# Six stages of a two-block transformer kernel, each with its moving tiles at another place in SBUF

## The reference, cut to what matters

```python
def swiglu(x, w_in, w_out):                       # twice, D_FF = 2816
    gate, up = jnp.split(x @ w_in, 2, axis=-1)
    return (jax.nn.silu(gate) * up) @ w_out

def sq_relu_mlp(h, up, down):                     # twice, D_FF_2 = 4096
    return jnp.square(jax.nn.relu(h @ up)) @ down

def conformer_conv(h, pw1, pw1_b, dw, dw_b, ln_w, ln_b, pw2, pw2_b):
    u = jax.nn.glu(h @ pw1 + pw1_b, axis=-1)
    ...                                           # 31 taps per channel, layer norm
    return jax.nn.silu(u) @ pw2 + pw2_b
```

## The kernel before

| tile | role | address | modulo 2048 |
|---|---|---|---|
| xn_hi, xn_lo | moving, up parts | 18560, 34944 | 128, 128 |
| w_hi, w_lo | stationary, block k of a slot at + 512 k | 67712, 84096 | 128 (then 640, 1152, 1664, 128, ...) |
| hid_hi, hid_lo | moving, down parts of all four layers | 125056, 157824 | 128, 128 |
| q_parts | queries; moving in the mixer's output product | 137344 | 128 |
| k_hi, k_lo | moving in the first mixer's scores | 170112, 182400 | 128, 128 |
| cy_hi, cy_lo | moving in pw2 | 125056, 141440 | 128, 128 |
| cu_hi, cu_lo | moving in the taps, first window | 162176, 166528 | 384, 640 |

## Time and profile before

### The profile page before, as it was taken

How to read it: one execution, slowest core, us unless ns; L and a number is a source line. 1 busy time by engine, 2 the same in 40 slices (tenths; PEclk the granted TensorE clock), 3 DMA queues, 4 the chain that set the end, 5 groups by cost and what they waited for, 6 DMA issues and landing times.

```text
span 2358.6 us, 36961 instructions
## 1 busy us (share of the span) xinstructions
PE 2303.7 (98%) x13968; PEld 1903.3 (81%) x13968; DVE 1165.4 (49%) x1781; ACT 910.2 (39%) x1444; POOL 1163.4 (49%) x685
## 2 busy tenths in 40 slices
PE   8999999999999999999999899999999999999998
PEld 7888887888888888878876678888888887888887
DVE  5432146268634421376554546723735986731632
ACT  5332125467743321265553314222233435222222
POOL 5444445554565454445374415444445983444442
PEclk9999999999999999999999989999999999999999
DMA  4323323310033333232110003332232232322321
GB/s 165 98 98 98 98 89 108 124 55 1 10 108 98 98 98 97 90 118 88 55 55 29 29 2 99 98 98 95 93 97 92 90 107 74 98 97 97 98 91 61
DMA packets 56125, 200.08 MB, mean 85 GB/s; under 512 B 6224, under 2 KB 6480, under 8 KB 56016
## 3 DMA queue, kind: packets, MB, share of 16 engines
q1 hardware_dynamic: 54432, 195.82, 25.7%
q10 hardware_dynamic: 1584, 2.75, 0.4%
HBM read 196.45 MB, written 2.10 MB: 84 GB/s over the span
## 4 chain that ended last, share of the span: by engine, by line
PE 50%; DVE 3%; ACT 1%; issue 0%; POOL 0%; DVEq 0%; POOLq 0%; ACTq 0%
PE ps L133 15%; PE ps L135 14%; PE ps L134 14%; PE ps L1997 1%; PE ps L640 1%; PE ps L1973 0%; DVE ps L2837 0%; PE ps L1993 0%; PE ps L655 0%; PE ps L1936 0%; PE ps L2044 0%; PE ps L1862 0%; DVE sb_aq L1002 0%; PE ps L1958 0%; DVE sb_ak_lo L1006 0%
## 5 line engine op out<-in xcount | busy, mean ns | idle before, releaser
L114 POOL TENSOR_TENSOR sb_w_lo<-sb_w_raw,sb_w_hi 128x1024 fp32r<-128x1024 f32 (+1 forms) x361 | 888.4, 2463 | 925.6 <-ACT sb_w_hi L101 923.9
L133 PE MATMUL ps<-sb_xn_hi,sb_w_hi 128*128 128x512 f32 x1688 | 666.5, 395 | 2.4 <-POOL sb_w_lo L224 2.4
L134 PE MATMUL ps<-sb_xn_lo,sb_w_hi 128*128 128x512 f32 x1688 | 658.1, 390 | 0.0
L135 PE MATMUL ps<-sb_xn_hi,sb_w_lo 128*128 128x512 f32 x1688 | 657.8, 390 | 0.0
L101 ACT ACTIVATE sb_w_hi<-sb_w_raw 128x1024 fp32r<-128x1024 f32 x362 | 380.4, 1056 | 476.6 <-PE ps L135 450.5
L133 PEld LDWEIGHTS ps<-sb_xn_hi,sb_w_hi 128*128 128x128 f32 x1688 | 316.6, 188 | 72.8 <-issue 3.6
L135 PEld LDWEIGHTS ps<-sb_xn_hi,sb_w_lo 128*128 128x128 f32 x1688 | 316.7, 188 | 67.6
L134 PEld LDWEIGHTS ps<-sb_xn_lo,sb_w_hi 128*128 128x128 f32 x1688 | 316.8, 188 | 66.2 <-issue 1.7
L133 PE MATMUL ps<-sb_hid_hi,sb_w_hi 128*128 128x512 f32 x864 | 336.3, 389 | 2.0 <-DVE sb_hid_lo L401 2.0
L135 PE MATMUL ps<-sb_hid_hi,sb_w_lo 128*128 128x512 f32 x864 | 336.1, 389 | 0.0
L134 PE MATMUL ps<-sb_hid_lo,sb_w_hi 128*128 128x512 f32 x864 | 336.1, 389 | 0.0
(11 more groups left out here) (444 smaller groups left out, 3010.2 us busy)
## 6 DMA issues: line engine op xcount, KB each, us to landing
sb_w_raw<-weights SPq DMA_DIRECT2D x365, 512.0 KB, 3.4
sb_stage<-x SPq DMA_DIRECT2D x4, 512.0 KB, 4.9
sb_abias<-table ACTq DMA_DIRECT2D x8, 256.0 KB, 3.8
out<-sb_out_stage SPq DMA_DIRECT2D x8, 256.0 KB, 2.9
sb_lora_w<-lora ACTq DMA_DIRECT2D x2, 256.0 KB, 2.8
sb_par<-params SPq DMA_DIRECT2D x1, 231.0 KB, 6.4
sb_ctaps<-dw ACTq DMA_DIRECT2D x1, 124.0 KB, 2.0
```

What stands on the lines that cost most here:

```text
L114: pool.tensor_tensor(c.w_lo[:, slot, 0:width], c.w_raw[:, slot, 0:width], c.w_hi[:, slot, 0:width].bitcast(F32), ALU.subtract).then_inc(c. ...
L133: pe.matmul(out, hi, rhs_hi(k0 + k), start=first, stop=False)
L134: pe.matmul(out, hi, rhs_lo(k0 + k), start=False, stop=False)
L135: mm = pe.matmul(out, lo, rhs_hi(k0 + k), start=False, stop=last)
```

## The change

Nothing is computed in another way and no instruction is added, removed or moved: each engine's list has the same operations, shapes and waits in the same order. What changes is where tiles lie. The four layers get hidden tiles of their own (`c.hid[name]`), which share one place in turn, each behind a gap of its own. `gate`, `h` and `out_stage` now stand ahead of the hidden tiles instead of behind them. A gap stands ahead of `q_parts` and one ahead of the convolution's tiles.

```diff
+HID_GAPS = (("ffn1", 1920), ("ffn2", 512), ("mlp0", 1024), ("mlp1", 64))
...
+    sb("gap_q", [P, 384])
     m.q = sb("q_parts", [P, 16, T], F32R)
...
+    sb("gap_cy", [P, 32])
     v.y_hi = sb("cy_hi", [P, KD, T], F32R)
...
-            c.hid_hi = sb("hid_hi", [P, F1A, T], F32R, region)
-            c.hid_lo = sb("hid_lo", [P, F1A, T], F32R, region)
             c.gate = sb("gate", [P, 2, T], scope=region)
             c.h = sb("h", [P, 2, T], scope=region)
             c.out_stage = sb("out_stage", [P, TT, D], scope=region)
+            c.hid = {}
+            for name, gap in HID_GAPS:
+                with ExitStack() as own:
+                    sb("gap_" + name, [P, gap // 4], scope=own)
+                    c.hid[name] = (sb(name + "_hid_hi", [P, F1A, T], F32R, own), sb(name + "_hid_lo", [P, F1A, T], F32R, own))
...
-                down_pe(pe, c, B[name + "_downA"], F1A, c.hid_hi, c.hid_lo, hid_ready(f))
+                down_pe(pe, c, B[name + "_downA"], F1A, *c.hid[name], hid_ready(f))
```

More of the change, by code:

```diff
@@ L378, in glu_up_act, with glu_up_dve @@
                 act.activation(c.gate[:, s // 2], c.ps[:, slot], ACT.Silu).then_inc(c.s_act, 1)
-def glu_up_dve(dve, c, base, nf, hid_base, act_base, free_pe):
+def glu_up_dve(dve, c, base, nf, hid_base, act_base, free_pe, hid):
     dve.wait_ge(c.s_pe, free_pe + START)
@@ L394, in glu_up_dve, with hidden_parts @@
             dve.wait_ge(c.s_evac, i * RING + (u + START + 1))
-            hidden_parts(dve, c, i, f, hid_base)
-def hidden_parts(dve, c, i, f, hid_base):
-    dve.tensor_copy(c.hid_hi[:, i * 2 + f], c.h[:, f]).then_inc(c.s_hhi, 1)
+            hidden_parts(dve, c, i, f, hid_base, hid)
+def hidden_parts(dve, c, i, f, hid_base, hid):
+    hid_hi, hid_lo = hid
+    dve.tensor_copy(hid_hi[:, i * 2 + f], c.h[:, f]).then_inc(c.s_hhi, 1)
     dve.wait_ge(c.s_hhi, i * 2 + (hid_base + f + 1))
-    dve.tensor_tensor(c.hid_lo[:, i * 2 + f], c.h[:, f], c.hid_hi[:, i * 2 + f].bitcast(F32),
+    dve.tensor_tensor(hid_lo[:, i * 2 + f], c.h[:, f], hid_hi[:, i * 2 + f].bitcast(F32),
                       ALU.subtract).then_inc(c.s_hid, 1)
@@ L2533, in mlp_up_act, with mlp_up_dve @@
             act.activation(c.gate[:, s % 2], c.ps[:, slot], ACT.Relu).then_inc(c.s_act, 1)
-def mlp_up_dve(dve, c, base, nf, hid_base, act_base):
+def mlp_up_dve(dve, c, base, nf, hid_base, act_base, hid):
+    hid_hi, hid_lo = hid
     dve.wait_ge(c.s_pe, base + START)
@@ L2546, in mlp_up_dve @@
             dve.wait_ge(c.s_evac, i * RING + (u + START + 1))
-            dve.tensor_copy(c.hid_hi[:, i * RING + s], c.h[:, s % 2]).then_inc(c.s_hhi, 1)
+            dve.tensor_copy(hid_hi[:, i * RING + s], c.h[:, s % 2]).then_inc(c.s_hhi, 1)
             dve.wait_ge(c.s_hhi, i * RING + (hid_base + s + 1))
-            dve.tensor_tensor(c.hid_lo[:, i * RING + s], c.h[:, s % 2], c.hid_hi[:, i * RING + s].bitcast(F32),
+            dve.tensor_tensor(hid_lo[:, i * RING + s], c.h[:, s % 2], hid_hi[:, i * RING + s].bitcast(F32),
                               ALU.subtract).then_inc(c.s_hid, 1)
@@ L3195, in ffn @@
                 up_pe(pe, c, B[name + "_upA"], 2 * F1A, KD * i, lambda: norm_pe(pe, c, i))
-                down_pe(pe, c, B[name + "_downA"], F1A, c.hid_hi, c.hid_lo, hid_ready(f))
+                down_pe(pe, c, B[name + "_downA"], F1A, *c.hid[name], hid_ready(f))
                 up_pe(pe, c, B[name + "_upB"], 2 * (F1 - F1A), KD * i, None)
-                down_pe(pe, c, B[name + "_downB"], F1 - F1A, c.hid_hi, c.hid_lo, hid_ready(f + F1A))
+                down_pe(pe, c, B[name + "_downB"], F1 - F1A, *c.hid[name], hid_ready(f + F1A))
             def mlp(name, f, i):
                 up_pe(pe, c, B[name + "_upA"], F1A, KD * i, lambda: norm_pe(pe, c, i))
-                down_pe(pe, c, B[name + "_downA"], F1A, c.hid_hi, c.hid_lo, hid_ready(f))
+                down_pe(pe, c, B[name + "_downA"], F1A, *c.hid[name], hid_ready(f))
                 up_pe(pe, c, B[name + "_upB"], F1A, KD * i, None)
-                down_pe(pe, c, B[name + "_downB"], F1A, c.hid_hi, c.hid_lo, hid_ready(f + F1A))
+                down_pe(pe, c, B[name + "_downB"], F1A, *c.hid[name], hid_ready(f + F1A))
             input_pe(pe, c)
@@ L3228, in ffn @@
                 norm_dve(dve, c, i)
-                glu_up_dve(dve, c, B[name + "_upA"], F1A, f, f, B[name + "_upA"])
+                glu_up_dve(dve, c, B[name + "_upA"], F1A, f, f, B[name + "_upA"], c.hid[name])
                 down_dve(dve, c, B[name + "_downA"], F1A, 0.5, scaled)
-                glu_up_dve(dve, c, B[name + "_upB"], F1 - F1A, f + F1A, f + F1A, B[name + "_upB"])
+                glu_up_dve(dve, c, B[name + "_upB"], F1 - F1A, f + F1A, f + F1A, B[name + "_upB"], c.hid[name])
                 layer_end_dve(dve, c, B[name + "_downB"], F1 - F1A, i + 1, 0.5, scaled + KD, following, gain_sq)
@@ L3235, in mlp @@
                 norm_squared_dve(dve, c, i)
-                mlp_up_dve(dve, c, B[name + "_upA"], F1A, f, f)
+                mlp_up_dve(dve, c, B[name + "_upA"], F1A, f, f, c.hid[name])
                 down_dve(dve, c, B[name + "_downA"], F1A, 1.0, scaled)
-                mlp_up_dve(dve, c, B[name + "_upB"], F1A, f + F1A, f + F1A)
+                mlp_up_dve(dve, c, B[name + "_upB"], F1A, f + F1A, f + F1A, c.hid[name])
                 layer_end_dve(dve, c, B[name + "_downB"], F1A, i + 1, 1.0, scaled + KD, following)
```

## The result

The changed kernel takes 2367.07 us (median of 16, 2364.96 to 2368.49) where the kernel before has 2360.33 us (median of 16, 2358.48 to 2363.63): a ratio of 1.0027, 95% interval 1.0020 to 1.0034. It is slower by 6.7 us, with 4.7 to 8.0 us as the interval. The time lies within the range of the prediction (2350 to 2369), but the forecast was no change, and the case that came true is rival (a), which had a chance of 0.20.

The account below looks back on a forecast made before the run. The prediction took TensorE, busy 2303.7 of 2358.6 us, as the bound. Its terms, 0 + 0 + 0 + 0 = 0 us on the profiled 2360.41 us, gave 2360.5 us, with a range of 2350 to 2369.

Parts of the forecast that it names:

- rival (a): ffn1, mlp1 and pw2 slow down where the distance is no multiple of 256: 2367 us, at most 2371.5; chance 0.20.
- The bound: Whole kernel: TensorE, busy 2303.7 of 2358.6 us; only its matmul pace and its few waits can move the time.
- regular pace: Long matmul stretches before the change: 226.7 ns per matmul, marked by recorded durations all 389 ns.
- The sorting by distance: Moved matmuls classed by moving tile's start minus weight block's, modulo 512; ffn2, mlp0, mixer's output product keep 0: 1488 matmuls, 0 us.
- the other class: ffn1, mlp1 and pw2, 1488 matmuls at new distances 384, 64 and 128: priced at 0 ns each, 0 us.
- the first tap: Convolution's first three tap matmuls, at distances 256 and 0: 0.68 us, read as the regular pace and nearest row to the changed stages.
- The rule on lines of 16 bytes: SBUF is read in 16-byte lines, so starts at any multiple of 16 cost the same: 0 us.
- the slow taps: Convolution taps from the second on, windows shifting by four bytes: 234 ns per matmul, read as agreeing with the 16-byte rule.
- the gate unit: Unit with weight blocks of 24 columns, never at the regular pace: 231 ns per matmul, 4.4 ns more.
- Rival (b): Another remainder has a pace below 226.7 ns: 2352.5 to 2356.5 us, put at 2354; chance 0.28.
- the uneven stretch: Nine matmuls after a stretch of short ones, 231 ns each with one 0.22 us distance, before settling into the regular pace.
- The small terms: Taps 0, up to 1.5 us either way; part borders 0.7 us at most; other engines 0, perhaps 0.6 us.

Follow-up runs that it names:

- same_class_half: Changed kernel with ffn1, mlp1 and the convolution put back at 128, keeping new places of ffn2, mlp0 and q_parts: 2361.34 us, ratio 1.0001 to the kernel before.
- The pair of shifts: Kernel before with 384 bytes ahead of all tiles: 2361.04 us, ratio 0.9996; kernel before with 384 bytes ahead of the weight tiles: 2404.0 us, ratio 1.0184.
- the sweeps: Three runs of the changed kernel with other gaps, distances in multiples of 64, then twice at odd multiples of 32 in the layers: 2372.46, 2377.46 and 2377.78 us.
- fine_4_8_16_48: Hidden tiles as views beginning 4 (ffn1), 8 (ffn2), 16 (mlp0) and 48 (mlp1) bytes past the weight blocks' remainder: 2377.86 us; kernel before 2361.18 us.
- sweep with 320: Changed kernel with other gaps, distances ffn1 192, ffn2 256, mlp0 320, mlp1 448, q_parts 128, pw2 384: 2372.46 us, ratio 1.0048.
- weights_shifted_384: Kernel before with a gap of 384 bytes ahead of the weight tiles, moving tiles of streamed products in place: 2404.0 us, ratio 1.0184.
- other_class_half: Changed kernel with ffn2, mlp0 and q_parts put back at 128, keeping new places of ffn1, mlp1 and the convolution: 2366.3 us, ratio 1.0022 to the kernel before.
- the one-operand experiments: High and low hidden tiles at different distances: 2365.91 us beside 2360.41; kernel before with w_lo alone moved 128 bytes: 2395.97 us, 34.8 us over.

## Why the prediction failed, step by step

**The bound held.** TensorE is busy for 2307.3 of 2363.9 us, and ffn1 and mlp1 lost without a wait more; pw2 has one more, 0.4 us for `w_lo` of GpSimd. The reading of the earlier trace rows as a regular pace with its mark of 389/389/389 held in the stages that kept it, through all experiments.

**The sorting by distance held.** ffn2, mlp0 and the mixer's output product cost nothing, as the sum said, and `same_class_half` shows it alone. The pair of shifts shows that the distance is the cause.

**The step that failed is the price of the other class:** "I therefore take 0 ns, so 0 us." The runs showed 6.6 ns for ffn1, 2.2 ns for mlp1 and about 5.8 ns for pw2, together 6.3 us. The row that I called nearest, the first tap at distances 256 and 0, was no evidence for 64, 128 and 384: the sweeps show that 256 and 0 are one and the same distance, since the scale repeats after 256. I had sorted modulo 512 and then took the only other member of the trace as a neighbour of the new ones when it was a twin of the old; rival (a) had sorted by multiples of 256, which is right. The rest of the evidence spoke for rival (a) as well: other places in the trace had left the regular pace with no wait.

**The rule on lines of 16 bytes** (the Trainium skill, "SBUF — State Buffer", Specifications (TRN2)) gave the same 0 us and doesn't cover this: a distance of 16 has 231.7 ns and one of 32 has 233.3 ns. So the slow taps, which I had read as agreeing with it, were no evidence for it. The other one that I weighed (the Trainium skill, "TensorE: Matmul & The Clock Gate", Part 2: loading the next weights takes nothing from the moving operand's read) doesn't carry what I drew from it, that the distance means nothing: moving the weight tiles alone cost 43 us. Whether a read is slowed by the other or something else makes the pace, no run shows. I had seen the row that spoke against it, the gate unit, and still priced the distance at nothing.

**Rival (a)** gave 2367 us and the time is 2367.07. Its condition is right: the pace is lost where the distance is no multiple of 256. Its picture, that the reads never fall into step, is not what the rows show: ffn1 alternates steadily, and at 192 every duration is 394 ns. So each distance has steady patterns of its own, and the gate unit's pace was no measure of them. By its own sign, 231 ns or more in both layers, ffn1 passes and mlp1 (228.9) doesn't. The size is right by luck: one price of 4.4 ns for 1488 matmuls gave 6.5 us, where 528 x 6.6 + 768 x 2.2 + 192 x 5.8 = 6.3 us, with ffn1 above and mlp1 below the price, and the ledger has 5.5. In pw2 the trace shows 0.5 us rather than 1.1, although the wait of 0.4 us is in it: its first matmuls, after an idle stretch of 3.8 us, are taken at the clock's lower level, 1.2 GHz, and fewer of them in the changed kernel (granted clock 0.72 in the 6 us around its start, against 0.54). Its point of decision, 3.2 ns per matmul, was passed on average at 4.2.

**Rival (b)**, a faster pace elsewhere, had 0.28, the larger chance of the two, and nothing supports it: of 15 new distances modulo 512 in steps of 32, 256 is equal and all others are slower, and 216 ns was reached nowhere. The row that it was priced from, a distance of 0.22 us in the uneven stretch, is within the rounding of the starts to 0.01 us. The same 0.22 us stands in the middle of the regular pace, where nothing is faster than 226.7 ns:

```profile
254.75 0.39 PE L134 MATMUL ps<-sb_hid_lo,sb_w_hi 128*128 128x512 f32 x1
254.97 0.39 PE L135 MATMUL ps<-sb_hid_hi,sb_w_lo 128*128 128x512 f32 x1
255.20 0.39 PE L133 MATMUL ps<-sb_hid_hi,sb_w_hi 128*128 128x512 f32 x1
```

Nor did (b)'s own sum, which ends at 2352.5 us, give a reason for the 0.12 that I put below 2350.

**The small terms** (other engines, borders of stages, taps) stayed small; `same_class_half` contains the first two and moved by 0.01%, and the stretch with the taps, from the end of mlp0 to pw2, has 154.4 us before and 154.5 after.

The rows gave no ground for so large a gap between the chance of "no change" (0.52) and that of rival (a) (0.20): the argument for 0 ns rested on one group of three matmuls, and three groups showed that a pace can be lost.

## What to carry to other kernels

If TensorE takes fp32r matmuls of 512 columns back to back, each with a new weight block of 128 columns, allot the tiles so that the moving tile and the weight block begin at the same address modulo 256. Then look at the pace: 226.7 ns, with 389 ns recorded for all three lines of the product, was the best that any distance gave here. Other shapes and types were not tried. Where all tiles lie together did not matter for the one common shift that was tried, so one remainder for all stages does, and a remainder for each stage gains nothing and can lose. When a trace has a single row from which a new case is priced, ask first in which modulus it is really another case.

## What the runs showed of the hardware

The pace of 512-column fp32r matmuls, each with a new weight block of 128 columns, by the distance from the weight block's start to the moving tile's, modulo 256:

| distance, bytes | ns per matmul | from |
|---|---|---|
| 0 (also 256) | 226.7 | before, after, sweeps |
| 4, 8, 16, 48 | 238.1, 232.5, 231.7, 233.3 | fine_4_8_16_48 (high tiles; low ones 256 further) |
| 32, 96, 224 | 233.3 (once 233.6) | two sweeps |
| 64 | 228.9 | after, sweep with 320 |
| 128 | 232.1 to 232.6, or 233.3 | weights_shifted_384, pw2 and q_parts in a sweep; ffn1 in after |
| 160 | 234.2, 234.4 | two sweeps |
| 192 | 233.3 | sweep, at 192 and 448 |

At 128 there are two steady patterns: the changed kernel's ffn1 alternates between 0.23 and 0.24 us, pw2 and the kernel with shifted weights go through a longer one. Which of them a stretch falls into is not set by the addresses alone: ffn1's second down part, with the same addresses in both, has 27.9 / 120 = 232.5 ns in the changed kernel and 28.7 / 123 = 233.3 ns in `other_class_half`:

```profile
L135 PE MATMUL ps<-sb_ffn_hid_lo,sb_w_hi x41: 390/393/404, 350.0 to 377.9; 128*128 128x512 f32 x41
...
L135 PE MATMUL ps<-sb_ffn_hid_lo,sb_w_hi x42: 392/395/398, 350.1 to 378.8; 128*128 128x512 f32 x42
```

So TensorE settles into a periodic state, of which the distance is one input. The other engines don't make the pattern: it goes on unbroken through the changed kernel's ffn1, while ScalarE, GpSimd and VectorE are busy for only 17.0, 38.6 and 13.5 of 89 us. What happens in it stays open: the one-operand experiments show only that the costs of operands don't add up, and that a weight block out of step costs more (231.1 ns with `w_lo` alone at 128) than a moving tile (228.9 ns).
